# C attention's probabilities turned by VectorE and a scratch array instead of TensorE, in a two-layer streaming encoder

## The chip, the cores and the metric

One core of a Trainium2 chip. The metric is the device time of one execution in microseconds (us); lower is better. TensorE multiplies matrices, VectorE, ScalarE and GpSimd work on SBUF and PSUM, SyncE (its DMA queue is "SP") issues most transfers.

## The reference

Two layers over x of 1024 rows and 2048 columns, float32. Each layer projects x to 5376 columns, runs three branches, gates each, projects back to 2048 columns, adds 1.41 x and normalises.

```python
h = einsum('bsd,de->bse', x, w_in)      # a_v a_gate b_q b_k b_v b_gate c_q c_k c_v c_gate
a = pool_mixer(a_v, a_group_w, a_scale) * silu(a_gate)              # windows 2/4/8/16
b = swa_sink_attention(b_q, b_k, b_v, b_sinks) * silu(b_gate)       # 16 heads, 2 chunks, sinks
c = chunk_relbias_attention(c_q, c_k, c_v, c_rel_bias) * silu(c_gate)
x = layer_norm(alpha * x + einsum('bse,ed->bsd', concat(a, b, c), w_out), gain, bias)
```

The branch that matters here is C: 8 heads of 64; each chunk of 64 rows attends to itself and the 8 chunks before it, softmax over (q k / 8 + bias of the clipped distance), then times the values.

## The kernel before

Float32 numbers are split into a high and a low part; a product is three matmuls (high x high, high x low, low x high). Work is done in four steps `it`: a layer in two halves of 512 rows (`half(it)` is 0 or 1). Columns run along the partitions; a "unit" is a weight block of 128 x 512 which feeds 12 matmuls (four 128-row tiles of x, three each). The units pass a ring of four slots: SP loads `raw` (`load_unit`), ScalarE makes `wh` (`split`, L974), GpSimd `wl` (L1340), TensorE uses them (`project`).

A step's first part is four "pairs" `p`, each with 24 units for one group of A and two heads of C: `quarter(0..24)` are A's values, C's values, C's keys, C's queries, A's gate, C's gate, four units each (unit 24 is the next pair's unit 0). Then come 8 units for B's first query and keys (`KV0`), B (`B0`), and the output projection (`O0`). The pairs are a hardware loop on every engine but GpSimd, the order of the instructions in it is written by hand for each engine, and semaphores order the engines.

C's attention runs in four steps j of 128 queries for each of the pair's two heads: `c_scores` (TensorE, into `sc[h]`), `c_max` (VectorE: near bias, maximum), `c_exp` (ScalarE, into `prob`), `c_normalise` (VectorE), `c_transpose` (TensorE, 128x128 blocks of `prob` back into `sc[h]`, L681), `c_hi` (ScalarE, from `sc[h]`) and `c_lo` (VectorE, from `sc[h]` less the high part) into `pt`, `c_attend` (TensorE, `pt` times the values into `c_out[j]`), `c_low_rows` (ScalarE) and `c_add` (VectorE). A first half sees 1, 2, 3, 4 blocks of 128 keys in steps 0 to 3, a second half always 5. On TensorE step 0's scores follow unit 16, and step 3's attend follows unit 24, all within the pair; scores j+1 wait for `c_lo` of step j, since both use `sc[h]`. C's last attend, `c_out[3]`, uses a bank of `sc[0]`.

In steps 1 to 3 VectorE also does the layer norm of the step before, a quarter of the columns in each pair: `centre` (after the turn of C's values), `gain_and_bias` (its gain and bias are loaded into `prob`), and in steps 1 and 2 `turn_rows` (transposes in 32x32 blocks, stored in 128-byte pieces). A's mixer is a chain of VectorE operations after `av_ok`. Behind the pairs VectorE rotates B's first query and keys (`rotate`), makes their low parts (`keys_lo`, `rotated_query`) and turns B's values (L1699), before which TensorE does not start B's scores.

Of the kernel before, what the change touches and what calls it, by code (L numbers as in the profile page):

```python
# [29 lines left out]
F32 = mybir.dt.float32  # L30
F32R = mybir.dt.float32r
ALU = mybir.AluOpType
# [22 lines left out]
TWOS = B_TILES // 2  # L55
C_KEYS = 640
# [22 lines left out]
O0 = B0 + B_TILES * U_B  # L79
U_STEP = O0 + 4 * U_N  # L80

# [22 lines left out]
def build(nc, x, x_t, wall, a_gw, a_scale, sinks, rel_rev, ln_gain, ln_bias, rope_cos, rope_sin,  # L104
          pool_coef, pool_inv, out):
    with ExitStack() as ctx:
# [19 lines left out]
        bval_d = nc.dram_tensor("b_values_scratch", (DEPTH, CHUNK + SEQ, P), F32, kind="Internal").ap()  # L126
        tz_d = nc.dram_tensor("bias_rows_scratch", (DEPTH * 8, P * TZ), F32, kind="Internal").ap()
# [20 lines left out]
        bq0 = sb("bq0", [P, CHUNKS, 2, CHUNK], F32R)  # L148
        pt = sb("pt", [P, 5, 2, 2, P], F32R)
# [32 lines left out]


# [58 lines left out]
        c_out = [pv[:, 0:512], pv[:, 512:1024], pv[:, 0:512], sc[0][:, 0:512]]  # L242
# [62 lines left out]
        hist_in = sem("hist_in")  # L305
# [7 lines left out]
        ct_full = sem("ct_full")  # L313
# [60 lines left out]
        def last_rows(t, a, b):  # L374

            return sums[:, 4 * t:4 * t + 4, :].rearrange("p c n -> p (c n)")[:, a:b]

# [21 lines left out]
        def _(sp):  # L399
# [98 lines left out]
            for it in range(STEPS):  # L498
                with sp.Fori(0, C_PAIRS) as p:
                    for s in range(U_C):  # L500
                        if s == (4 if it else 0):

                            sp.wait_ge(gwl_ok, p + (C_PAIRS * it + 1))
                            sp.dma_start(gw[:], a_gw[layer(it), ds(p, 1)].rearrange("o c d -> (o c) d")
                                         ).then_inc(gw_in, 16)
                        if s == 9 and half(it):

                            sp.wait_ge(w_used, unit(it, p * U_C) + (2 + RING))
                            for m, a, b in ((mixh, 0, 3), (mixl, 3, 6)):
                                sp.dma_start(m[:, MIX_B:MIX_B + 2 * (b - a) - 1:2, :].bitcast(F32),  # L510
                                             hist_d[ds(p, 1), :, a:b, :].rearrange("o p a n -> (o p) a n")
                                             ).then_inc(hist_in, 16)
                        if s == 10:

                            sp.wait_ge(bias_ok, p + (C_PAIRS * it + 1))
                            if it:
                                sp.wait_ge(rope_ok, (B_TILES + 1) * it)
                                sp.wait_ge(bt_full, 2 * B_TILES * it)
                            else:
                                sp.wait_ge(tz_out, p * (16 * DEPTH) + 16 * DEPTH)  # L520
                            sp.dma_start(brope[:, 0, :].rearrange("p (h n) -> p h n", h=2),
                                         tz_d[ds(2 * p + 8 * layer(it), 2), 127:127 + P * (TZ - 1)]
                                         .rearrange("h (q c) -> q h c", c=TZ - 1)[:, :, 0:NEAR]).then_inc(bias_in, 16)
                        if s == 8 and it:

                            sp.wait_ge(w_used, unit(it, p * U_C) + (1 + RING))
# [1394 lines left out]
```

## Time and profile before

| | us |
|---|---|
| median of 3 runs | 2826.12 (2825.72 to 2827.51) |
| profiled execution | 2824.71 |
| its span | 2822.9 |
| TensorE busy | 2807.9 (99%) |
| VectorE busy | 1762.0 (62%) |
| ScalarE busy | 1297.4 (46%) |
| GpSimd busy | 1277.3 (45%) |
| DMA moved | 384.49 MB, 136 GB/s |

TensorE's granted clock was full in all 40 slices of the span. A row of a group gives what it wrote and read, the number of instructions, busy us and mean ns of one, then the idle time of the engine before them and who ended it. TensorE's matmuls are pipelined: one of 512 columns is listed with 0.39 us and the next starts 0.23 us later, so costs on TensorE are read from start to start.

### The profile page before, as it was taken

What the parts mean: (1) busy time and instruction counts of PE and PEld (TensorE: products, weight loads), DVE (VectorE), ACT (ScalarE), POOL (GpSimd) and SP (SyncE); (2) the same over time, 40 slices, a digit from 0 to 9 for tenths busy, and PEclk for the clock granted to TensorE, in tenths of its full rate; (3) what the DMA queues carried; (4) which work ended last, traced back from release to release, by engine and by line L of the source; (5) the groups of instructions that cost most, each with busy time, mean ns of one, the idle gap of its engine ahead of it and who ended that gap; (6) DMA issues with size and microseconds to landing.
All of it is one profiled execution on the core that took longest, in us unless ns stands there. A gap on an engine that the chain in (4) does not pass through costs nothing.

```text
span 2822.9 us, 45252 instructions
## 1 busy us (share of the span) xinstructions
PE 2807.9 (99%) x13316; PEld 2352.1 (83%) x13316; DVE 1762.0 (62%) x2950; ACT 1297.4 (46%) x2685; POOL 1277.3 (45%) x927
## 2 busy tenths in 40 slices
PE   9999999999999999999999999999999999999998
PEld 7888888888888888888888888888888888888886
DVE  5555679623777777862266666895137766678625
ACT  5444466523444445652244444664235444456521
POOL 4444444444444434444444444444444444444441
PEclk9999999999999999999999999999999999999999
DMA  6444332355555533335565663324564454333442
GB/s 212 132 133 131 100 89 82 112 175 176 169 168 167 162 91 98 86 94 179 172 192 172 174 173 105 86 82 133 155 214 133 129 155 151 100 86 84 136 157 101
DMA packets 311957, 384.49 MB, mean 136 GB/s; under 512 B 129408, under 2 KB 149920, under 8 KB 308128
## 3 DMA queue, kind: packets, MB, share of 16 engines
q1 hardware_dynamic: 308048, 367.26, 44.2%
q10 hardware_dynamic: 3792, 15.73, 1.4%
q8 instruction: 66, 1.08, 0.2%
q14 instruction: 51, 0.42, 0.0%
HBM read 327.23 MB, written 58.81 MB: 137 GB/s over the span
## 4 chain that ended last, share of the span: by engine, by line
PE 99%; DVE 0%; DMA 0%; issue 0%; ACT 0%; POOL 0%; SPq 0%; POOLq 0%
PE acc L639 70%; PE sc L639 18%; PE pv L639 9%; PE sc L681 2%; PE sc L718 1%; DMA raw<-in_wall 0%; DVE last_sums L1840 0%; DVE last_sums L1839 0%; POOL wl L1340 0%; DVE xl L1373 0%; SPq L489 0%; DVE av L1811 0%; DVE last_sums L1820 0%; ACT wh L974 0%; ACT xh L974 0%
## 5 line engine op out<-in xcount | busy, mean ns | idle before, releaser
L1340 POOL TENSOR_TENSOR wl<-raw,wh 128x512 fp32r<-128x512 f32 x920 | 1276.5, 1391 | 1501.9 <-ACT wh L974 1499.9
L974 ACT ACTIVATE wh<-raw 128x512 fp32r<-128x512 f32 x920 | 575.6, 630 | 1053.1 <-PE acc L639 722.3
L639 PE MATMUL acc<-xh,wh 128*128 128x512 f32 x2624 | 1034.0, 394 | 1.2 <-DVE xl L1373 1.2
L639 PE MATMUL acc<-xh,wl 128*128 128x512 f32 x2624 | 1022.7, 390 | 0.0
L639 PE MATMUL acc<-xl,wh 128*128 128x512 f32 x2624 | 1022.6, 390 | 0.0
L639 PEld LDWEIGHTS acc<-xh,wl 128*128 128x128 f32 x2624 | 492.6, 188 | 105.4
L639 PEld LDWEIGHTS acc<-xh,wh 128*128 128x128 f32 x2624 | 493.2, 188 | 98.2 <-DVE xl L1373 2.0
L639 PEld LDWEIGHTS acc<-xl,wh 128*128 128x128 f32 x2624 | 493.6, 188 | 94.0
L1373 DVE TENSOR_TENSOR xl<-prob,xh 128x512 f32 x48 | 55.6, 1158 | 235.8 <-ACT xh L974 235.8
L639 PE MATMUL sc<-wh,mixh 128*128 128x512 f32 x496 | 193.5, 390 | 0.1
L639 PE MATMUL sc<-wl,mixh 128*128 128x512 f32 x496 | 193.0, 389 | 0.0
L639 PE MATMUL sc<-wh,mixl 128*128 128x512 f32 x496 | 193.0, 389 | 0.0
L1373 DVE TENSOR_TENSOR pt<-sc,pt 128x512 fp32r<-128x512 f32 (+3 forms) x192 | 120.1, 663 | 80.7 <-ACT pt L974 79.7
L974 ACT ACTIVATE pt<-sc 128x512 fp32r<-128x512 f32 (+3 forms) x192 | 104.1, 577 | 82.2 <-PE sc L718 43.8
L1026 ACT ACTIVATE prob<-sc,nmax 128x640 f32<-128x640 f32 (+4 forms) x128 | 84.8, 662 | 71.9 <-DVE nmax L1426 70.0
L639 PEld LDWEIGHTS sc<-wh,mixh 128*128 128x128 f32 x496 | 93.1, 188 | 19.6 <-POOL wl L1340 0.5
L639 PEld LDWEIGHTS sc<-wh,mixl 128*128 128x128 f32 x496 | 93.1, 188 | 19.4
L639 PEld LDWEIGHTS sc<-wl,mixh 128*128 128x128 f32 x496 | 93.2, 188 | 19.1
L639 PE MATMUL acc<-wh,mixh 128*128 128x512 f32 x256 | 100.0, 391 | 0.0
L639 PE MATMUL acc<-wh,mixl 128*128 128x512 f32 x256 | 99.7, 389 | 0.0
L639 PE MATMUL acc<-wl,mixh 128*128 128x512 f32 x256 | 99.7, 389 | 0.0
L639 PE MATMUL pv<-wh,mixh 128*128 128x512 f32 x240 | 93.4, 389 | 0.0
(217 smaller groups left out, 3577.4 us busy)
## 6 DMA issues: line engine op xcount, KB each, us to landing
raw<-in_wall SPq DMA_DIRECT2D x920, 256.0 KB, 2.7
res_scratch<-res ACTq DMA_DIRECT2D x12, 1024.0 KB, 4.2
res<-res_scratch SPq DMA_DIRECT2D x12, 1024.0 KB, 4.9
res<-in_x SPq DMA_DIRECT2D x8, 1024.0 KB, 7.3
x_scratch<-res SPq DMA_DIRECT2D x8, 1024.0 KB, 5.2
x_t_scratch<-turned SPq DMA_DIRECT2D x128, 64.0 KB, 2.6
prob<-x_t_scratch SPq DMA_DIRECT2D x32, 256.0 KB, 2.8
res<-x_scratch SPq DMA_DIRECT2D x8, 1024.0 KB, 6.2
```

The source lines that it names most:

```text
L639: return nc.tensor.matmul(o, lhsT, rhs, start=start, stop=stop)
L681: last = nc.tensor.transpose(sc[h][:, cs], prob[:, h, cs], ident[:])
L718: last = nc.tensor.transpose(b_sc[g][:, u, c, :], probs(v, g)[:, u, c, :], ident[:])
L974: return nc.scalar.activation(o, i, ACT.Copy, scale=scale)
L1026: nc.scalar.activation(prob[:, h, c0:C_KEYS], sc[h][:, at:at + C_KEYS - c0], ACT.Exp, bias=nmax[:, h, 0:1], accum_out=psums[:, h, 0:1]).th ...
L1340: nc.gpsimd.tensor_tensor(wl[:, s, :], raw[:, s, :], wh[:, s, :].bitcast(F32), ALU.subtract).then_inc(w_lo, 1)
L1373: return V.tensor_tensor(o, whole, hi.bitcast(F32), ALU.subtract)
```

## The change

C's probabilities are no longer transposed on TensorE. VectorE turns `prob` in 32x32 blocks in place; SP stores it to a scratch array in DRAM with the blocks in their new places, one of four stores for each 32 partitions, and loads it again as `pt_raw` (the place of the low part in `pt`); `c_hi` and `c_lo` read `pt_raw`. The scores' banks are free after the exponents. A pair's four steps are spread: scores 0, 1, 2 follow units 16, 19 and 22, attend 0 follows unit 23; scores 3 follow unit 1 of the next pair, attends 1, 2, 3 its units 3, 6 and 10. The last pair's end lies among the first units of B. The loops over pairs are unrolled on all engines. The old keys and values of the second half are loaded by separate transfers; gain and bias are loaded at slot 13 of SP, behind the stores of step 3; gain and bias are applied as two operations with C's last sum between them.

```diff
+STORE_AT = (26, 29, 32, 36)
+LOAD_AT = (28, 31, 35, 38)
+        cprob_d = nc.dram_tensor("c_prob_scratch", (2, C_KEYS, P), F32, kind="Internal").ap()
+        pt_raw = nc.alloc_sbuf_tensor_at("pt_raw", [P, 5, 2, 2, P], F32, offset=pt_at)[:, :, :, 1, :]
-        c_out = [pv[:, 0:512], pv[:, 512:1024], pv[:, 0:512], sc[0][:, 0:512]]
+        c_out = [pv[:, 0:512], pv[:, 512:1024], pv[:, 0:512], pv[:, 512:1024]]
...
+            def store_c_prob(it, p, j, h):
+                n = c_step(it, p, j)
+                if n:
+                    sp.wait_ge(cp_in[h], 16 * n)
+                sp.wait_ge(cs_prob, 2 * n + h + 1)
+                c0 = 0 if half(it) else 512 - P * j
+                for r in range(4):
+                    rows = slice(32 * r, 32 * (r + 1))
+                    sp.dma_start(cprob_d[h, c0:C_KEYS, rows].rearrange("(m a) b -> a m b", a=32),
+                                 prob[rows, h, c0:C_KEYS].rearrange("a (m b) -> a m b", b=32)).then_inc(cp_out[h], 16)
+            def load_c_prob(it, p, j, h):
+                n = c_step(it, p, j)
+                sp.wait_ge(cp_out[h], 64 * (n + 1))
+                if n:
+                    sp.wait_ge(c_pv, n)
+                b0 = 0 if half(it) else 4 - j
+                sp.dma_start(pt_raw[:, b0:5, h, :], cprob_d[h, b0 * P:C_KEYS, :].rearrange("(c k) q -> k c q", k=P)
+                             ).then_inc(cp_in[h], 16)
+            def load_gain_bias(it, n):
+                if n:
+                    for h in range(2):
+                        sp.wait_ge(cp_out[h], 64 * c_step(it + 1, n, 0))
...
                 for h in range(2):
-                    pe.wait_ge(ct_lo, p * 8 + (8 * C_PAIRS * it + 2 * j + h + 1))
+                    if c_step(it, p, j):
+                        pe.wait_ge(cs_exp, 2 * c_step(it, p, j) + h - 1)
-            def c_transpose(it, p, j):
...
-                        last = nc.tensor.transpose(sc[h][:, cs], prob[:, h, cs], ident[:])
...
+                        quarter(1, 0)
+                        if p:
+                            c_scores(it, p - 1, 3)
+                        quarter(2, 0)
+                        quarter(3, 0)
+                        if p:
+                            c_attend(it, p - 1, 1)
...
+                    if p:
+                        c_attend(it, p - 1, 3)
+                    quarter(11, 0)
...
                     c_scores(it, p, 0)
+                    for s in range(17, 20):
+                        quarter(s, 0)
                     c_scores(it, p, 1)
...
+                    c_scores(it, p, 2)
                     quarter(23, 1)
+                    if half(it):
+                        pe.wait_ge(hist_values_in, p * 32 + (32 * C_PAIRS * layer(it) + 32))
+                    pe.wait_ge(v_ok, p + ((C_PAIRS + 1) * it + 1))
+                    c_attend(it, p, 0)
...
+                    if n:
+                        act.wait_ge(cp_out[h], 64 * n)
+                    act.wait_ge(cs_max, 2 * n + h + 1)
...
-                    copy(pth[:, b0:5, h, :], sc[h][:, b0 * P:5 * P].rearrange("p (b q) -> p b q", q=P)).then_inc(ct_hi, 1)
+                    act.wait_ge(cp_in[h], 16 * (c_step(it, p, j) + 1))
+                    copy(pth[:, b0:5, h, :], pt_raw[:, b0:5, h, :]).then_inc(ct_hi, 1)
...
+                    slot(22)
+                    slot(23)
+                    c_hi(it, p, 0)
+                    slot(24)
                     c_exp(it, p, 2)
                     mix_hi(p * 2 + (nb + 1), p + MIX_A)
+                    c_low_rows(it, p, 0)
...
-                    V.tensor_scalar(prob[:, h, c0:C_KEYS], prob[:, h, c0:C_KEYS], rinv[:, h, 0:1], None, ALU.mult
-                                    ).then_inc(cs_prob, 1)
+                    V_(V.tensor_scalar(prob[:, h, c0:C_KEYS], prob[:, h, c0:C_KEYS], rinv[:, h, 0:1], None, ALU.mult))
+                    V.transpose(prob[:, h, c0:C_KEYS], prob[:, h, c0:C_KEYS]).then_inc(cs_prob, 1)
...
+                    lo(ptl[:, b0:5, h, :], pt_raw[:, b0:5, h, :], pth[:, b0:5, h, :]).then_inc(ct_lo, 1)
```

VectorE's order in a pair is now: maximum 3 and c_lo 1 of the pair before, small copies, normalise 3, c_add 1, c_lo 2, the mixer's chain, c_add 2, the turn of C's values, centre, the mixer's low part, c_lo 3, the bias's preparation, gain, c_add 3 and C's product, bias, C's mix_lo, the keys' low part, turn_rows, values, queries, maximum 0, normalise 0, maximum 1, A's gate, normalise 1, c_lo 0, A's product, maximum 2, A's mix_lo, normalise 2, c_add 0, C's gate. Behind the last pair it is: maximum 3, c_lo 1, normalise 3, c_add 1, c_lo 2, rotate, c_add 2, the query's low part, rotate, c_lo 3, c_add 3, product, old keys, mix_lo, then keys_lo and the rest as before.

## Rows read from the trace of the kernel before

**Rows 1.** The page: the chain that ended last, shares of the span by line

```profile
PE acc L639 70%; PE sc L639 18%; PE pv L639 9%; PE sc L681 2%; PE sc L718 1%; DMA raw<-in_wall 0%; DVE last_sums L1840 0%; DVE last_sums L1839 0%; POOL wl L1340 0%; DVE xl L1373 0%; SPq L489 0%; DVE av L1811 0%; DVE last_sums L1820 0%; ACT wh L974 0%; ACT xh L974 0%
```

**Rows 2.** TensorE's groups by form: busy us, mean ns, idle before them

```profile
L681 PE MATMUL sc<-ident,prob 128*128 128x128 f32 x480 | 63.3, 273 | 0.0
```

**Rows 3.** Timeline of TensorE, pair 1 of step 1: start us, us, instructions

```profile
844.29 1.25 PE L681 MATMUL sc<-ident,prob 128*128 128x128 f32 x10
845.30 0.48 PE L639 MATMUL acc<-mixh,bq 128*128 128x512 f32 x1
845.61 0.40 PE L639 MATMUL acc<-mixl,bq 128*128 128x512 f32 x1
```

**Rows 4.** Three pairs of steps 0 and 1: us, then PE, PEld, DVE, ACT, POOL busy

```profile
84.70:304.80 220.10, 220.10 (x1043) 184.11 (x1042) 125.06 (x256) 99.38 (x201) 93.85 (x72) 1.00 0.45 130
778.25:1018.99 240.74, 240.74 (x1210) 204.72 (x1210) 176.75 (x301) 114.87 (x204) 106.03 (x72) 1.00 0.53 154
```

**Rows 5.** The chain in order of time: 16 units of TensorE

```profile
858.49 43.55 PE acc L639 x192
```

**Rows 6.** Timeline of VectorE, pair 2 of step 1

```profile
859.87 1.73 DVE L1406 TENSOR_TENSOR c_att<-c_low 64x128 f32<-64x128 f32 x2
...
868.00 1.56 DVE L1586 TENSOR_TENSOR s<-av 128x527 f32<-128x527 f32 x1 [3.65 <-ACT av L974]
...
874.70 0.28 DVE L1373 TENSOR_TENSOR bq<-gw,bq 128x128 fp32r<-128x128 f32 x1
...
878.23 3.01 DVE L1527 TENSOR_SCALAR res<-res,mv,rstd 128x512 f32<-128x512 f32 x4
881.57 1.38 DVE L1373 TENSOR_TENSOR mixl<-s,mixh 128x512 fp32r<-128x512 f32 x1 [0.32 <-ACT mixh L974]
...
893.74 2.49 DVE L1544 STREAM_TRANSPOSE turned<-res 128x512 f32<-128x512 f32 x4
...
902.71 0.11 DVE L1422 MEMSET sc<- 64x64 f32 x1 [1.32 <-PE sc L639]
...
905.54 0.15 DVE L1432 RECIPROCAL rinv<-psums 128x1 f32<-128x1 f32 x1
905.73 0.56 DVE L1433 TENSOR_SCALAR prob<-prob,rinv 128x640 f32<-128x640 f32 x1
...
933.91 0.68 DVE L1403 TENSOR_TENSOR c_low<-pv,c_low 64x512 f32<-64x512 f32 x1
934.63 0.59 DVE L1406 TENSOR_TENSOR c_att<-c_low 64x128 f32<-64x128 f32 x2
935.25 1.56 DVE L1373 TENSOR_TENSOR pt<-sc,pt 128x640 fp32r<-128x640 f32 x2
```

**Rows 7.** Timeline of GpSimd in the same pair

```profile
859.85 1.29 POOL L1340 TENSOR_TENSOR wl<-raw,wh 128x512 fp32r<-128x512 f32 x1 [1.53 <-ACT wh L974]
```

**Rows 8.** Timeline of ScalarE in the same pair

```profile
930.68 0.80 ACT L1026 ACTIVATE prob<-sc,nmax 128x640 f32<-128x640 f32 x1 [1.46 <-DVE nmax L1426]
...
935.44 0.63 ACT L974 ACTIVATE mixh<-tmp 128x512 f32 x1
```

**Rows 9.** Timeline of VectorE behind the pairs of step 1

```profile
1024.46 2.74 DVE L1671 CAST b_keys<-b_keys 128x64 fp32r<-128x64 f32 x4
...
1044.18 4.86 DVE L1373 TENSOR_TENSOR b_keys<-s,b_keys 64x512 fp32r<-64x512 f32 x4 [2.75 <-ACT b_keys L974]
1049.15 0.69 DVE L1514 SCALAR_TENSOR_TENSOR s<-acc,brope 128x512 f32<-128x512 f32 x1
...
1059.95 0.72 DVE L1699 STREAM_TRANSPOSE tmp<-sc 128x512 f32<-128x512 f32 x1 [3.46 <-PE sc L639]
```

**Rows 10.** SP's issues in that pair; engines meanwhile (last columns: DMA share, GB/s)

```profile
899.86 4.20 SPq L469 DMA_DIRECT2D x_t_scratch<-turned  x8
...
895.00:903.00 8.00, 8.00 (x40) 6.79 (x39) 3.53 (x9) 3.08 (x5) 3.72 (x4) 1.00 1.02 278
```

**Rows 11.** The page: DMA issues, KB each, median us from issue to landing

```profile
x_t_scratch<-turned SPq DMA_DIRECT2D x128, 64.0 KB, 2.6
```

More of the change, by code:

```diff
@@ L312, in build @@
         cs_prob = sem("cs_prob")
-        ct_full = sem("ct_full")
+        cp_out = [sem(f"cp_out{h}") for h in range(2)]
+        cp_in = [sem(f"cp_in{h}") for h in range(2)]
         ct_hi = sem("ct_hi")
@@ L1112, in pair @@
                     else:
-                        for s in range(2, 5):
-                            slot(s)
+                        slot(2)
+                        if p:
+                            c_hi(it, p - 1, 1)
+                        slot(3)
+                        if p:
+                            c_exp(it, p - 1, 3)
+                        slot(4)
                     used(it, p * U_C + (6 if first else 3))
@@ L1572, in _, with c_tail_product @@
                 pc, nb = C_PAIRS * it, 16 * it
-                per_c = 27 + (2 if it else 0) - half(it)
-                with dv.Fori(0, C_PAIRS) as p:
-                    section(p * per_c + total)
+                def c_tail_product(p, values):
+                    dv.wait_ge(c_fold, c_step(it, p, 3) + 1 + 2)
+                    attention_product(p * 2 + (MIXES * it + 2), values)
+                for p in range(C_PAIRS):
+                    section(total)
+                    if p:
+                        c_max(it, p - 1, 3)
+                        c_lo(it, p - 1, 1)
                     V.tensor_copy(coef1[:], coef[:, ds(p, 1), :].rearrange("p o n -> p (o n)"))
@@ L1583, in _ @@
                         V_(V.memset(av[:, 0:16], 0.0))
+                    if p:
+                        c_normalise(it, p - 1, 3)
+                        c_add(it, p - 1, 1)
+                        c_lo(it, p - 1, 2)
                     dv.wait_ge(av_ok, p + (pc + 1))
@@ L1624, in _ @@
                     if it:
-                        gain_and_bias()
-                        low_keys()
+                        gain()
+                    if p:
+                        c_add(it, p - 1, 3)
+                        c_tail_product(p - 1, p + (pc + 1))
+                    if it:
+                        bias()
+                    if p:
+                        mix_lo(p * 2 + nb, p - 1 + MIX_C)
+                    low_keys()
                     if turns(it):
@@ L1667, in _ @@
+                dv.wait_ge(rope_in, 32 * (it + 1))
+                rotate(it, 0, KV0 + 3, 0)
+                c_add(it, p, 2)
+                rotated_query(ROTS * it + 1, 0)
+                rotate(it, 1, KV0 + 7, 1, 1.0)
+                c_lo(it, p, 3)
+                c_add(it, p, 3)
+                c_tail_product(p, C_PAIRS * (it + 1))
                 dv.wait_ge(prod_ok, MIXES * it + 2 * C_PAIRS + 2)
```

318 lines of the change are left out of this document (160 added, 158 removed).

## Prediction, made before the changed kernel was run

> **What bounds the kernel now.** First the chain of work that ended last, by line: it is all TensorE's matmuls, 2% of it the transposes of L681 [rows 1]. Then the busy time of each engine over three C pairs: TensorE is busy in all of it (240.74 of 240.74 us), so it never waits inside the loops; a pair takes 73.4 us in the first half of the sequence (220.1 / 3) and 80.2 in the second half, and VectorE is busy 177 of 241 us in step 1 [rows 4]. (A step is one half of the sequence in one layer; steps 1 and 3 are second halves.) So time is won only where an instruction leaves TensorE, and lost where TensorE has to wait. Then TensorE's groups by form, for the 480 transposes of C [rows 2], and last the timelines of VectorE, ScalarE and GpSimd in one pair, since the question is who is late once TensorE is quicker.
>
> **What TensorE gets back.** Ten transposes of a second-half step of attention take 1.01 us from their start to the next matmul's, and that one lasts 0.31 us to the following start, where 0.23 is usual (a unit of 12 matmuls takes 43.55 / 16 = 2.72 us [rows 5]): 1.10 us. There are 32 such: 35.2 us [rows 3]. In a first half a pair has 20 transposes in four runs: by the same 0.10 each and 0.09 for a switch 2.4 us, in eight pairs 18.9. Together 54.1 us, which the chain's 2% bears out. The other matmuls stay in number and form; scores and attends stand apart now, at 0.01 to 0.09 us for a switch, and the transposes' own switches go: zero. Were all else hidden, the profiled execution would take 2824.7 - 54.1 = 2770.6 us (its span is 2822.9, and 1.8 lies around it); the median of the runs is 1.4 above it.
>
> **What is added.** VectorE gets 64 transposes of 128x640 in second halves and 64 smaller ones: four of 128x512 take 2.49 us now [rows 6], so 0.78 for 640, or by a whole single one 0.85; I take 0.85. The low part c_lo now comes from two SBUF tensors. From PSUM two of 640 took 1.56 us [rows 6]; two adds of c_att, with two SBUF inputs, took 0.59 us in one place and 1.73 in another [rows 6], and in the other GpSimd's split of a weight ran from 859.85 for 1.29 us [rows 7]. So such an operation of VectorE waits while GpSimd runs one: c_lo costs between nothing more and 1.3 us more for each split it meets. The Trainium skill has the rule ("SBUF — State Buffer", section "SBUF: two separate sides": the port pair that both share is an exclusive lock held for the whole instruction); the trace agrees, and the rule speaks against taking c_lo's input out of PSUM. ScalarE's high parts keep their size, but they wait for cp_in and the exponents for cp_out, and behind those on ScalarE stand the weights' splits: rival 3. SP issues 8 stores (0.52 us each, 4.20 for 8 [rows 10]) and 2 loads more for each step of attention, and waits for cs_prob with the units' loads behind it, some 5 us. A load is issued some four units ahead of its split and the splits run three units ahead of TensorE, so 5 us delay neither; without that cover each would be a us of TensorE. Gain and bias of the norm share prob, so their load moves behind the stores of step 3; centre, which needs them, comes some 15 us later: hidden, else it adds to the last attend. Unrolling: TensorE runs through the pair boundary without a gap now, so between 0 and 5 us for code that is fetched; I take 0.
>
> **Who is late: the attend of step 1.** Scores and attend take 1.2 us each in a second half: (80.25 - 24 x 2.72 - 4.4 - 0.7 for three more matmuls) / 8. Count from the end of unit 22. TensorE: scores 2, unit 23, attend 0, units 24 and 1, scores 3, units 2 and 3: attend 1 is wanted at 3 x 1.2 + 5 x 2.72 = 17.2, its second head at 17.8. VectorE and ScalarE: the split of unit 26 0.63 [rows 8], then GpSimd's 1.29, which c_lo(0) meets, so it starts at 1.95: +1.56 is 3.5; A's product 0.7, 4.2; maximum of step 2, 2.83 (902.71 to 905.54 [rows 6]), 7.0; its second exponent 0.8 and mix_hi 0.63 [rows 8], 8.5; mix_lo 0.7, 9.1; normalise 2 x (0.19 + 0.56 + 0.85) = 3.2, 12.3; c_add 1.34 (933.91 to 935.25), 13.7; gate 0.7, 14.4; maximum of step 3 2.83, 17.2; c_lo(1) 1.56, 18.8. That is 1.0 us late; with one split met on the way (+0.7, normalise under the split of slot 25) 1.7. It comes once in each of 8 second-half pairs: 13.6 us. In a first half the same chain with smaller blocks ends about 1 us before it is wanted: 0.
>
> **The attend of step 3.** From the end D of c_lo(1), VectorE: four small copies 0.35, normalise 3.2, c_add 1.34, c_lo(2) 1.56, the mixer's chain 6.7 (868.00 to 874.70), gw 0.3, c_add 1.34, turn of values 0.7, centre 3.0, ya_l 1.3, c_lo(3) 1.56: D + 21.3 [rows 6]. TensorE: second head of attend 1 0.6, units 4 to 7 10.9, attend 2 1.2, units 8 to 10 8.2: wanted at D + 20.9, the second head at D + 21.5. Undisturbed it just fits. But five groups in it (normalise, both c_add, both c_lo) can meet a split, which fills 1.3 of 2.7 us: some 0.4 us each, 2 us in all, so 1.8 us late. That holds for pairs 1 to 3 of the two second halves (only step 0 has no centre): 6 x 1.8 = 10.8 us. In step 2 the same sum with smaller blocks gives 0.7 us: 3 x 0.7 = 2.1. In step 0 nothing.
>
> **The tail of a step.** Pair 3's last attends now lie among B's first projections. After attend 3, VectorE has the wait for c_low 0.6, c_add 1.4, product 0.7, in a second half the key copies 2.74, the wait for ScalarE's keys 2.75, keys_lo 4.86, then rotation and sinks 7.34 (1049.15 until it was free, 3.46 before 1059.95), and the turn of B's values 0.7 [rows 9]: 21.1 us. TensorE needs that turn after B3, four value units and one quarter, 6 x 2.72 = 16.3: 4.8 us late; in a first half, mix_hi in place of the key copies, 19.0, 2.7 late. Now VectorE waits 3.46 us there, because keys_lo lies early. Two of each: 15.0 us.
>
> **Sum.** 2824.7 - 54.1 + 13.6 + 10.8 + 2.1 + 15.0 = 2812.1; with 1.4 for the median 2813.5. Forecast 2814; its own range, 0.6 us either way in each of 21 places, is 2801 to 2828.
>
> **Rivals.** (1) Both attends are in time and only the tail is late: 2826.1 - 54.1 + 15.0 = 2787 (2772 to 2801). For it: the chains are late by 1 to 2 us after a dozen terms, and splits may fall between VectorE's operations, as at 934 us [rows 6]. Against: 1.0 us of the first chain needs no split. (2) Slower: GpSimd's splits decide. If each chain meets one more whole split, (8 + 9 + 4) x 1.3 = 27 us, 2841 (2828 to 2856). For it: the mixer's first operation takes 1.56 us, the c_att adds 1.73 [rows 6], and much of what VectorE gets is of this kind. From 0.6 us more in each place on the change is slower than before. (3) The way through the scratch array is late. Normalised heads come out 7 and 9 us after the start of scores 0, eight issues bring SP to 11, landing takes 2.6 us for 64 KB [rows 11] and as much again for the load: 17 to 19 us, while ScalarE reads it at 20. The stores are 655 KB in 128-byte pieces; where such stores run now the engines' share is 1.02 at 278 GB/s [rows 10], so 2.4 us or more. If it is 3 us over in 8 second-half pairs, 24 us: 2838. The Trainium skill ("DMA: Bandwidth & Descriptors", section "Specifications") puts transfers under 512 bytes off line rate, as read-modify-writes; the rows show them only mixed with weights. (4) That the change saves TensorE nothing is out: the transposes are gone from its program.
>
> **Chances.** Forecast 0.43, rival 1 0.24, rival 2 0.19, rival 3 0.12, rest 0.02. A measurement of this kernel can tell 0.2%, 5.7 us, from no change: faster is under 2820.5, slower over 2831.8. Of the forecast's 0.43, 0.30 lies under and 0.13 between. Faster 0.30 + 0.24 = 0.54, same 0.13 and 0.02 of rivals 2 and 3, slower 0.31. Eight in ten need both sides: 2783 to 2848.
>
> **What would show it.** L681 gone, and C's transposes on VectorE at 0.85 us. Idle time of TensorE before matmuls out of pt, released by VectorE's L1373, 26 us in all: 1.7 in attend 1 of second-half pairs, near 2 in their attend 3, none in step 0. Idle time before B's first scores, released by VectorE's turn, 2.7 and 4.8 us. Periods of second-half pairs of 79.3 us in place of 80.2, VectorE busy some 69 us in them. Wrong if the periods are 75.9 (rival 1), if attends wait over 3 us behind a long c_lo (rival 2), or if ScalarE's reads of pt_raw wait for DMA (rival 3).

## The result, and the profile of the changed kernel

The changed kernel takes 2905.6 us (median of four runs, 2904.6 to 2910.3) against 2826.0 for the kernel before on the same chip: a ratio of 1.0284, 95% interval 1.0266 to 1.0302. It is 80 us slower, where 2814 was forecast and the range ended at 2848. The profiled execution has a span of 2908.2 us against 2822.9, and the rest goes by these two.

The page of the changed kernel: busy times, TensorE's slices, DMA packets, the chain by engine and by line (its first entries are those of [rows 1]), and the DMA issues (KB each, median us to landing).

```profile
PE 2789.8 (96%) x12836; PEld 2317.0 (80%) x12836; DVE 1883.3 (65%) x3078; ACT 1279.8 (44%) x2676; POOL 1283.6 (44%) x927
...
PE   8888999999988999999999999999999998999998
...
DMA packets 629706, 448.10 MB, mean 154 GB/s; under 512 B 385665, under 2 KB 467617, under 8 KB 625825
...
PE 75%; DVE 8%; DMA 8%; SPq 5%; issue 3%; ACT 1%; POOL 1%; ACTq 0%; POOLq 0%; DVEq 0%
...
c_prob_scratch<-prob SPq DMA_DIRECT2D x256, 80.0 KB, 2.3
pt_raw<-c_prob_scratch SPq DMA_DIRECT2D x64, 320.0 KB, 4.9
```

TensorE's group of transposes [rows 2] is gone and it still idles 2908.2 - 2789.8 = 118 us, where it idled 15 (all but 3 us of that behind its last matmul). The chain was TensorE alone in [rows 1]; a quarter of it is something else now, DMA and SP's queue 13%. There are 385665 packets under 512 B; the kernel before had 129408.

The changed kernel's waits: engine, line, for whom; us in total, times, longest.

```profile
ACT pt L1029 <- DMA pt_raw<-c_prob_scratch: 87.8, 40, 6.5
PE pv L697 <- DVE pt L1450: 80.5, 33, 7.8
...
ACT wh L1029 <- DMA raw<-in_wall: 76.8, 22, 12.0
...
ACT prob L1084 <- DMA c_prob_scratch<-prob: 61.1, 42, 3.8
```

TensorE stands before its attends for VectorE's low part, which stands for ScalarE's high part, which stands for the load out of the scratch array. That is the third rival's sign. Two stretches show how. First step 0, pair 1, in the timelines of SP, ScalarE (with its queue) and TensorE, in one window (PE, PEld, DVE, ACT, POOL busy, then clock, DMA share, GB/s), and in the DMA view of 107 to 111 us (median us to landing of what is issued there):

```profile
97.91 9.20 SPq L475 DMA_DIRECT2D c_prob_scratch<-prob  x8
107.15 2.79 SPq L428 DMA_DIRECT2D raw<-in_wall  x2
110.03 7.99 SPq L485 DMA_DIRECT2D pt_raw<-c_prob_scratch  x2
118.07 0.97 SPq L428 DMA_DIRECT2D raw<-in_wall  x2
...
97.84 3.78 ACTq L1160 DMA_DIRECT2D bias_rows_scratch<-bias_row_scratch  x2
...
118.85 0.63 ACT L1029 ACTIVATE wh<-raw 128x512 fp32r<-128x512 f32 x1 [11.47 <-DMA raw<-in_wall]
...
122.18 1.19 PE L697 MATMUL pv<-pt,mixh 128*128 128x256 f32 x4 [7.37 <-DVE pt L1450]
...
109.00:127.00 18.00, 10.63 (x45) 8.74 (x44) 5.92 (x12) 4.04 (x7) 3.99 (x4) 0.81 0.58 161
...
raw<-in_wall SPq DMA_DIRECT2D x2, 256.0 KB, 11.0
pt_raw<-c_prob_scratch SPq DMA_DIRECT2D x1, 256.0 KB, 10.6
c_prob_scratch<-prob SPq DMA_DIRECT2D x1, 64.0 KB, 12.7
```

The eight stores take SP 9.2 us where 4.2 had been measured [rows 10], and one of them is 12.7 us on its way; the second head's load has to wait for it. The weights issued next, at 107.15, land at 118.8, and ScalarE waits 11.5 us for them; the first head's load, issued behind them at 110.03, lands at 120.7, and TensorE's attend, which waits 7.4 us, hangs on that. In this stretch the granted clock is 0.81: behind the wait matmuls start 0.43 us apart for a few us (the 1.2 GHz level) where 0.23 is usual. Such stretches cost some 13 us in the whole run (each start's excess over 0.227 us, added up). The DMA view of the same stretch, 97 to 119 us, in 40 slices:

```profile
DMA  9967987541161116211621166998731111111112
GB/s 326 210 179 220 178 157 152 104 93 48 46 144 54 48 48 137 61 46 48 142 56 45 48 78 150 406 342 267 239 100 48 46 48 48 46 48 50 48 51 96
...
raw<-in_wall SPq DMA_DIRECT2D x4, 256.0 KB, 7.2
...
pt_raw<-c_prob_scratch SPq DMA_DIRECT2D x2, 256.0 KB, 7.2
```

The engines are not full there. In about half of the slices they are busy to 0.1 at some 48 GB/s, one or two of sixteen, while everything is awaited. (The two medians of 7.2 us are the middle of landings of 10 to 12 us and of some 4 us for what is issued when the broadcast ends.)

Second, step 1, pair 2, timelines of SP, ScalarE, VectorE and TensorE, then the DMA view of 886 to 909 us:

```profile
899.39 2.42 SPq L485 DMA_DIRECT2D pt_raw<-c_prob_scratch  x2
901.86 2.17 SPq L428 DMA_DIRECT2D raw<-in_wall  x1
908.01 4.40 SPq L475 DMA_DIRECT2D c_prob_scratch<-prob  x8
...
915.69 0.43 SPq L499 DMA_DIRECT2D prob<-in_ln_bias  x1
...
908.02 0.74 ACT L1029 ACTIVATE pt<-pt_raw 128x640 fp32r<-128x640 f32 x1 [6.52 <-DMA pt_raw<-c_prob_scratch]
...
908.79 1.77 DVE L1450 TENSOR_TENSOR pt<-pt_raw,pt 128x640 fp32r<-128x640 f32 x2 [5.76 <-ACT pt L1029]
...
921.80 1.92 DVE L1604 TENSOR_SCALAR res<-res,mv,rstd 128x512 f32<-128x512 f32 x4 [2.84 <-DMA prob<-in_ln_bias]
...
909.76 0.87 PE L697 MATMUL pv<-pt,mixh 128*128 128x256 f32 x5 [3.55 <-DVE pt L1450]
```

```profile
q1 hardware_dynamic: 9634, 5.66, 87.9%
...
pt_raw<-c_prob_scratch SPq DMA_DIRECT2D x2, 320.0 KB, 8.8
```

Here the queue is full (88% of 16 engines' time) with stores in 128-byte pieces, 1 MB of the norm's rows, 1 MB of history keys and the bias rows, and the load lands after 8.8 us.

### The profile page after: what moved, and what is told of

The parts are those of the page before. It is cut to its first block, busy times and chain, and to the rows that moved or that the text cites. A ratio compares the mean times of both kernels' runs of the same rounds, so it can differ in the third digit from the quotient of the medians.

```text
span 2908.2 us, 41599 instructions
## 1 busy us (share of the span) xinstructions
PE 2789.8 (96%) x12836; PEld 2317.0 (80%) x12836; DVE 1883.3 (65%) x3078; ACT 1279.8 (44%) x2676; POOL 1283.6 (44%) x927
## 2 busy tenths in 40 slices
DMA packets 629706, 448.10 MB, mean 154 GB/s; under 512 B 385665, under 2 KB 467617, under 8 KB 625825
## 4 chain that ended last, share of the span: by engine, by line
PE 75%; DVE 8%; DMA 8%; SPq 5%; issue 3%; ACT 1%; POOL 1%; ACTq 0%; POOLq 0%; DVEq 0%
PE acc L697 50%; PE sc L697 15%; PE pv L697 9%; DMA pt_raw<-c_prob_scratch 3%; SPq L475 3%; DMA prob<-in_ln_bias 1%; DVE mixl L1450 1%; DMA raw<-in_wall 1%; DMA c_prob_scratch<-prob 1%; PE sc L766 1%; SPq L428 1%; SPq L513 1%; DVE pt L1450 1%; POOL wl L1417 1%; DVE prob L1512 0%
## 5 line engine op out<-in xcount | busy, mean ns | idle before, releaser
L1450 DVE TENSOR_TENSOR pt<-pt_raw,pt 128x640 fp32r<-128x640 f32 (+4 forms) x128 | 98.2, 798 | 91.8 <-ACT pt L1029 90.5
L697 PE MATMUL pv<-pt,mixh 128*128 128x256 f32 x240 | 45.2, 312 | 77.8 <-DVE pt L1450 77.8
L1029 ACT ACTIVATE pt<-pt_raw 128x640 fp32r<-128x640 f32 (+4 forms) x128 | 72.7, 596 | 98.2 <-DMA pt_raw<-c_prob_scratch 87.8
L697 PEld LDWEIGHTS pv<-pt,mixh 128*128 128x128 f32 x240 | 36.8, 206 | 93.6 <-issue 92.0
L697 PEld LDWEIGHTS sc<-wh,mixh 128*128 128x128 f32 x496 | 93.1, 188 | 19.6 <-POOL wl L1417 0.5
```

The source lines that it names most:

```text
L697: return nc.tensor.matmul(o, lhsT, rhs, start=start, stop=stop)
L1029: return nc.scalar.activation(o, i, ACT.Copy, scale=scale)
L1450: return V.tensor_tensor(o, whole, hi.bitcast(F32), ALU.subtract)
```

## The experiments

The last four columns say what each step costs against the kernel before, from the start of the last unit of each step in the two profiled executions (us); the first is the median's distance from the kernel before on the same chip, and the four add up to it within some 6 us.

| kernel | against before | step 0 | 1 | 2 | 3 |
|---|---|---|---|---|---|
| changed kernel | +79.7 | +30.5 | +20.8 | +15.9 | +18.6 |
| no way through the array | +6.2 | +17.5 | -1.8 | -3.5 | -3.3 |
| one large store a head | +22.3 | +24.6 | -1.8 | -2.7 | +2.3 |
| four large stores a head | +45.8 | +23.6 | +7.4 | +12.4 | +2.9 |
| stores without loads | +24.8 | +27.1 | -4.1 | +4.8 | -2.8 |
| bias rows early | +62.1 | +12.6 | +19.0 | +13.9 | +18.7 |
| bias rows early, two arrays | +48.3 | +13.1 | +13.6 | +10.2 | +12.7 |
| broadcast spread | +47.7 | -2.0 | +15.8 | +19.6 | +16.4 |
| spread, two arrays | +36.3 | -3.7 | +14.7 | +11.7 | +9.4 |
| no way, spread | -14.4 | -3.9 | -1.6 | -3.5 | -3.2 |

**Is it the way through the array?** Theory: rival 3, the transfers. Rival: VectorE is late (rivals 1 and 2). First the changed kernel without them:

```diff
-    sp.dma_start(cprob_d[...], prob[...]) x4; sp.dma_start(pt_raw[...], cprob_d[...])
-    copy(pth[:, b0:5, h, :], pt_raw[:, b0:5, h, :])
+    copy(pth[:, b0:5, h, :], pt[:, b0:5, h, 1, :].bitcast(F32))    # same size, constant
```

> The changed kernel without the way through DRAM: no store of the turned probabilities and no load of pt_raw, c_hi and c_lo read the low part's place in pt instead (so C's probabilities are wrong numbers), the exponents wait for the normalising of the step before. VectorE's transposes and its c_lo from SBUF stay. Theory 1 (what cost the 80 us is the way through the scratch array and SP's queue): the waits of attends 2 and 3 for it go, VectorE's own lateness as I summed it stays, 2805 to 2835 us. Theory 2 (VectorE's added work and its collisions with GpSimd): the time stays above 2885 us. Between 2835 and 2885 both have a share.

2832.3 us, ratio 1.0019 (1.0009 to 1.0028). That is in the range of theory 1. So 73 of the 80 us are the transfers, and steps 1 to 3 come out below the kernel before. Step 0 stays at +17.5.

**Which part of the way?** Large pieces in the same region and of the same size, first as one store a head, then as four:

```diff
-                for r in range(4):
-                    rows = slice(32 * r, 32 * (r + 1))
-                    sp.dma_start(cprob_d[h, c0:C_KEYS, rows].rearrange("(m a) b -> a m b", a=32), ...
+                sp.dma_start(cprob_d[h, c0:C_KEYS, :]....rearrange("(p n) -> p n", p=P), prob[:, h, c0:C_KEYS])
```

> The changed kernel with one store for each head, of the same bytes to the same region, in rows of 512 to 2560 bytes for each partition in place of four stores in 128-byte pieces (so the probabilities come back in wrong places). Loads and all waits stay. If the small pieces and SP's eight issues make the way late: about half of the loss comes back, 2850 to 2870 us. If it is the latency of two transfers and the order of SP's queue, whatever the pieces: above 2890 us.

> The changed kernel with its four stores per head kept in number, bytes and place, but each moving 32 whole rows of prob into one contiguous piece of the scratch array, so no piece is 128 bytes; what is loaded back is therefore not the turned block. Theory A, the pieces: the time is that of the run with one large store per head, 2848 us (2843 to 2856), SP's four more issues a head costing nothing that TensorE sees. Theory B, the issues: SP takes about 0.5 us for each, its loads of weights stand behind, and most of the 57 us between the changed kernel and the large single store stays: 2885 to 2905. Between the two, each us over 2848 goes to the issues.

2848.4 and 2872.1 us (1.0076, 1.0059 to 1.0092; 1.0168, 1.0151 to 1.0185). The first is 2 us below the range for small pieces and issues together; the second lies between its two theories, which share the price. A ladder: transfers in one large store 16 us, four issues in place of one 24, pieces of 128 bytes in place of large ones 34. Then the stores alone:

```diff
-                    sp.wait_ge(cp_in[h], 16 * n)
+                    sp.wait_ge(cp_out[h], 64 * n)
...
-                sp.dma_start(pt_raw[:, b0:5, h, :], cprob_d[h, b0 * P:C_KEYS, :]...
...
-    copy(pth[:, b0:5, h, :], pt_raw[:, b0:5, h, :])
+    copy(pth[:, b0:5, h, :], pt[:, b0:5, h, 1, :].bitcast(F32))
```

> The changed kernel without the 64 loads out of the scratch array: c_hi and c_lo read a constant block in place of what came back, all stores of 128-byte pieces stay, and the exponents still wait for their landing. The run with neither is 2832 us, the changed kernel 2905. Theory A, the way through the array is late (store, landing, load, landing, one after the other): most of the 73 us goes with the loads, 2840 to 2860, and what stays is the exponents' wait for prob. Theory B, the stores harm by what they do to the others (SP's queue, weights' loads behind them, the engines' read-modify-writes): 2880 to 2900, TensorE's waits then moving to units whose weights are late.

2850.9 us (1.0091, 1.0075 to 1.0108), theory A. In steps 1 to 3 stores alone cost nearly nothing (-4.1, +4.8, -2.8 against -1.8, -3.5, -3.3): what costs there are the loads, 57 of the 61 us that they add to the span lying in those three steps. By the waits above that is because they come back late; this run alone does not part that from what stands behind them in SP's queue. In step 0 the stores alone cost 10.

Then the gain and bias load that was moved behind the stores, left out, so that the norm multiplies by and adds what lies in prob:

```diff
                     if s == 13 and it:
-                        load_gain_bias(it - 1, p)
+                        pass
```

> The changed kernel without the two broadcast loads of the norm's gain and bias, so centre waits for its input rows alone and gain and bias multiply by what lies in prob. Waits of TensorE before attend 3 in steps 1 to 3 are 23.7 us in all in the changed kernel and 5.1 us without the way through the scratch array. Theory A, centre is late because this load stands behind the landing of the fourth step's stores: the waits fall to some 8 us, 2890 (2884 to 2895). Theory B, attend 3 is late because its own blocks come late out of the scratch array: 2902 to 2906, no change. Step 0 keeps its time under both.

2899.3 us (1.0264, 1.0247 to 1.0281): 6 us, at neither theory's number, and no more than the two intervals leave open. centre has no wait left (VectorE stood 19 us for it in all), but TensorE's waits before attends are 77.7 us in all where they were 80.5, and many are still 2.6 to 3.6 us. In pair 2 of step 1 the load for attend 3 now lies there in time (landed at 919.3, wanted by VectorE at 922.2); what stays is attend 2's wait for its load, and VectorE's chain that starts late behind it. The moved load was not hidden from VectorE, but it was not the cause.

**Step 0.** There ScalarE's queue issues the broadcast of the next pair's bias rows. Issue it behind slot 17 of the pair before:

```diff
-                        if it == 0:
-                            bias_rows()
...
                     slot(17)
+                    if it == 0 and p + 1 < C_PAIRS:
+                        act.wait_ge(bias_in, 16 * (p + 1))
+                        bias_rows(p + 1)
```

> The changed kernel, where in step 0 ScalarE's queue issues the broadcast of a pair's bias rows some 12 units earlier, away from the stores of the fourth attention step; nothing else is altered. In the changed kernel step 0 costs 30.5 us more than in the kernel before, 7.5 us of it in each of pairs 1 to 3 at the attend of step 3, with landing of the stores taking up to 12.7 us while the broadcast runs. Theory A, the broadcast holds up the stores: those waits fall under 2 us each, 17 to 22 us less: 2884 to 2889. Theory B, the 128-byte pieces and SP's issues do it alone: 2900 to 2910, waits of 7 us as before. The other steps keep their times under both.

2888.4 us (1.0223, 1.0196 to 1.0250), theory A: step 0 falls from +30.5 to +12.6, the others stay. The four runs of this kernel lie from 2881.3 to 2898.4, so the total is loose; the steps are those of an execution at the median. SP's eight stores take 4.21 us again:

```profile
102.21 4.21 SPq L475 DMA_DIRECT2D c_prob_scratch<-prob  x8
```

The other suspect in step 0 was a move that the prediction overlooked: the keys' low part (low_keys) now stands behind VectorE's wait for the bias rows in step 0 too. In the kernel without the way, VectorE and TensorE in pair 0:

```profile
54.55 0.62 DVE L1700 TENSOR_SCALAR brope<-brope 128x256 f32<-128x256 f32 x2 [13.32 <-DMA brope<-bias_rows_scratch]
...
58.14 0.80 PE L681 MATMUL acc<-xh,wh 128*128 128x512 f32 x1 [4.12 <-DVE mixl L1436]
```

Undone in the changed kernel, without the way, and with the early broadcast:

```diff
+                    if it == 0:
+                        low_keys()
                     dv.wait_ge(bias_in, p * 16 + (16 * pc + 16))
...
-                    low_keys()
+                    if it:
+                        low_keys()
```

> The changed kernel with one move undone: in step 0 VectorE makes the keys' low part before it waits for the bias rows, as in the kernel before. The wait of TensorE before unit 16 in pair 0 of step 0 (4.1 us) should go: 2901 (2898 to 2904) if the later pairs, in which the wait for attend 3 covers it, keep their times; 2895 if the shorter way of VectorE helps them too. Rival: the keys are not late for this move but because VectorE itself is late; then 2905 and the wait stays at 4.

> The run without the way through the scratch array (2832 us), with one more move undone: in step 0 VectorE makes the keys' low part before it waits for the bias rows. Left out are the stores and loads of the scratch array, so the second products are not of the turned block. In that run TensorE waits 4.12, 2.04, 2.69 and 2.73 us before unit 16 of the four pairs of step 0, released by VectorE's low part of the mixed keys. Theory A, these are the price of that move: 11.6 us of waits and some 6 us of matmuls at half clock behind them go, 2815 to 2821, which is the blind forecast's 2814 without its transfers. Theory B, VectorE is late in step 0 anyway and the wait moves to another place (attend 1 or 3, or the bias rows' maximum): 2828 to 2833. With the changed kernel itself the same move gained 0 to 6 us, since there the waits for the fourth step lay behind it.

> The whole changed kernel with both moves: bias rows broadcast some 12 units earlier in step 0, and the keys' low part made ahead of the wait for them. With the first alone 2888 us. Theory A, what is left of step 0 is then the wait of 4.25 us before unit 16 and its matmuls at half clock: 2881 to 2885. If the two add to nothing, 2888. Neither can reach the 2826 of the kernel before, since the steps 1 to 3 keep their 55 us.

2905.1, 2818.2 and 2892.1 us. Without the way it gives 14 us (0.9970, 0.9960 to 0.9980) as theory A had it. In the changed kernel it gives nothing. That is the rival's time, though not for the rival's reason, for TensorE's wait of 4 us in pair 0 does go. With the early broadcast it gives nothing either (2881 to 2888 had been expected): other waits of step 0 take its place. But both step 0 findings hang on one thing, that the bias rows land late, and the DMA view above says why. The broadcast is issued with the two heads as the outer dimension. One pattern turned round, nothing moved:

```diff
-    act.dma_start(tz_d[heads].rearrange("h (q c) -> h q c", c=TZ),
-                  rel_d[heads].rearrange("h (o c) -> h o c", o=1).to_broadcast([2, P, TZ])
+    act.dma_start(tz_d[heads].rearrange("h (q c) -> q h c", c=TZ),
+                  rel_d[heads].rearrange("h (o c) -> o h c", o=1).to_broadcast([P, 2, TZ])
```

> The changed kernel with one address pattern altered: the broadcast of a pair's bias rows (two issues by ScalarE's queue, same bytes, same place in the order) runs over the 128 copies first and the two heads second, in place of the heads first. In the changed kernel the engines' share is 0.1 at 46 to 48 GB/s for most of 12 us while it runs, about two of the sixteen, and loads issued meanwhile land after 7.2 us in place of 2.8. Theory A, two engines do the broadcast and all other transfers wait for their part on those two: spread over sixteen it takes 1 to 3 us, the three waits of 7.4 to 7.8 us in step 0 go, 2883 to 2890, as with the broadcast issued earlier, and SP's eight stores issue in some 4 us in place of 9.2. Theory B, what crowds is the 128-byte pieces and the amount of data: 2900 or more.

2873.8 us (1.0161, 1.0143 to 1.0179), 32 us less, more than theory A asked. ScalarE's queue is through with the two issues in 1.22 us where it took 3.78, the broadcast's packets run for 5 us (95.9 to 101.2) where they ran for 20 (99.3 to 119.1), and the DMA view of the same stretch (96 to 118 us) shows it:

```profile
94.58 1.22 ACTq L1160 DMA_DIRECT2D bias_rows_scratch<-bias_row_scratch  x2
```

```profile
DMA  6998799996476799599999999993069899884000
...
raw<-in_wall SPq DMA_DIRECT2D x7, 256.0 KB, 3.6
pt_raw<-c_prob_scratch SPq DMA_DIRECT2D x2, 256.0 KB, 4.0
```

In the pairs of step 0 TensorE has no wait of 0.3 us or more left once the first 11 us are over, with the stores in 128-byte pieces and the moved low_keys in place: pairs 1 to 3 gain 2.2 to 2.3 us each on the kernel before, where the prediction gave 2.4 for 20 transposes. One detail went otherwise: SP's eight stores still took 7.6 us there, so the narrowness of the broadcast alone is not what makes them slow to issue. The Trainium skill ("DMA: Bandwidth & Descriptors", section "Why a DMA increments its semaphore by 16 and not by 1") says that a transfer is spread over the largest number of engines up to 16 that divides the outermost dimension of both sides: two heads, two engines. The trace agrees, at 46 to 48 GB/s and a share of 0.1. The kernel before has the same narrow broadcast, 20 us long, but could not gain by this turn: its TensorE waits 3 us in all, in the first 10 us of the run.

**Steps 1 to 3.** Two scratch arrays in turn, so that a store need not wait for the last load's landing (upon the early broadcast):

```diff
-                if n:
-                    sp.wait_ge(cp_in[h], 16 * n)
+                if n > 1:
+                    sp.wait_ge(cp_in[h], 16 * (n - 1))
-    cprob_d[h, ...]
+    cprob_d[2 * (n % 2) + h, ...]
```

> The whole changed kernel with the bias rows broadcast earlier (2888 us), and the scratch array doubled: steps of attention take turns, so a store waits for the load of the step before the last and not for the last one, which was issued one unit ahead of it and takes 4.9 to 8.6 us. Theory A, SP's waits for that landing (42 us in the changed kernel, 28 of them) delay the next stores and with them the next load: without them loads land 2 to 4 us earlier, TensorE's waits before attends 2 and 3 in steps 1 to 3 (some 30 us) fall by half, 2868 to 2878. Theory B, the length of the way itself decides (eight issues, landing, load, landing), and SP only waits there in place of later: 2883 to 2893.

2874.9 us (1.0170, 1.0153 to 1.0187), theory A in the total: 13.5 us less, nearly all of it in steps 1 to 3. SP's waits of that kind, in the changed kernel and here:

```profile
SPq L475 <- DMA pt_raw<-c_prob_scratch: 42.1, 28, 4.7
```

```profile
SPq L475 <- DMA pt_raw<-c_prob_scratch: 7.5, 20, 1.2
```

Then, upon that, the loads of the history keys and of the bias rows two units later, behind the third load:

```diff
-                    if s == 10 and half(it):
+                    if s == 12 and half(it):
...
-                    if s == 10:
+                    if s == 12:
```

> The run with two scratch arrays and the early broadcast (2875 us), with the loads of the history keys (two of 512 KB) and of the bias rows (256 KB) issued two units later in every pair, behind the load of the third attention step and not ahead of it. Theory A, in steps 1 and 3 the third load is late because it stands behind these: it lands in 4 to 6 us in place of 8.8, and TensorE's waits before attend 2 (0.6 to 2.2 us in 6 places) go: 2866 to 2872. Rival, the keys or the bias rows are then late themselves, or attend 3 waits longer by as much: 2873 to 2880.

2905.8 us (1.0284, 1.0266 to 1.0302), 31 us worse, worse than the rival said. The bias rows are then late themselves; VectorE stands for them 13 us in step 0, and keys and attends stand behind it in every step:

```profile
132.61 0.62 DVE L1714 TENSOR_SCALAR brope<-brope 128x256 f32<-128x256 f32 x2 [13.16 <-DMA brope<-bias_rows_scratch]
```

The order that was tried only changed who waits. The sums of these steps:

> The whole changed kernel with the broadcast spread (at its own place), two scratch arrays and the history keys and bias rows two units later. If each mends what it is for: 2860 to 2870. The lower end is set by the run without any transfer of the scratch array, 2832; the kernel before is at 2826, which this cannot reach.

> As the one before it, and in step 0 the keys' low part ahead of the wait for the bias rows. Without any transfer that move gained 14 us, with the early broadcast it lost 4 (within its spread). With a broadcast that no longer holds up the loads it should gain some of it: 2850 to 2860; if exponents still wait for the stores' landing in step 0, as they did with the early broadcast, nothing: 2860 to 2870.

> The whole changed kernel with the broadcast of the bias rows spread over the copies (2874 us alone) and two scratch arrays in turn (13 us less where the broadcast was merely early). Theory A, they act in different steps and add: 2859 to 2865, step 0 without a wait of TensorE in its pairs. Theory B, the spread broadcast leaves nothing for the second array to mend: 2870 to 2875. Under both it stays slower than the 2826 of the kernel before.

2893.0, 2881.0 and 2862.3 us. The first missed its range by 23 us and the second by 11 to 21; both carry the later keys, and the third, which differs from the first in that alone, is 31 us faster. Between the first two the undone low_keys gives 12 us, since the bias rows are late again there. The third, 1.0141 (1.0119 to 1.0163), has its median at theory A, but its runs lie from 2856.6 to 2872.6, so that how much the second array adds to the spread broadcast is loose. It is the best whole form of the change that was found, still 36 us behind the kernel before. None beats it.

**The blind sum without transfers.** Last, neither stores nor loads, and the broadcast spread:

> The changed kernel with neither stores nor loads of the scratch array (their second products are not of the turned block) and the broadcast spread. The keys' low part stays behind the wait for the bias rows, as in the change. Theory A, that move costs only because the narrow broadcast lands late: its waits of 2.0 to 4.1 us before unit 16 go without undoing it, step 0 ends at -5 to -7 us against the kernel before, and the whole is 2808 to 2814, the blind forecast's 2814 or a little under. Theory B, the move costs by itself: 2825 to 2832.

2811.7 us (0.9949, 0.9932 to 0.9965), theory A; step 0 ends at -3.9 where -5 to -7 had been expected. TensorE in step 0's tail, before attends 1 and 3 in step 1 and in that step's tail, and a window of one pair:

```profile
342.65 0.73 PE L681 MATMUL sc<-b_keys,bq 128*128 128x128 f32 x4 [1.89 <-DVE tmp L1786]
...
854.37 0.83 PE L681 MATMUL pv<-pt,mixh 128*128 128x256 f32 x5 [1.63 <-DVE pt L1436]
...
876.80 0.82 PE L681 MATMUL pv<-pt,mixh 128*128 128x256 f32 x5 [0.62 <-DVE pt L1436]
...
1053.93 1.22 PE L681 MATMUL sc<-b_keys,bq 128*128 128x256 f32 x4 [2.97 <-DVE tmp L1786]
...
771.10:849.60 78.50, 76.25 (x364) 64.05 (x364) 67.03 (x109) 36.61 (x67) 34.40 (x24) 1.00 0.56 159
```

**Two halves of the change by themselves.** In the kernel before, TensorE's transposes left out (the high and low parts are taken from the scores where they lie), and, in another kernel, VectorE's transposes added behind normalise with everything else kept (what TensorE then turns is already turned in blocks):

```diff
-    c_transpose: up to five transposes by ident a head
+    c_transpose: its waits and its signal alone
```

```diff
-    V.tensor_scalar(prob[...], prob[...], rinv[:, h, 0:1], None, ALU.mult).then_inc(cs_prob, 1)
+    V_(V.tensor_scalar(prob[...], prob[...], rinv[:, h, 0:1], None, ALU.mult))
+    V.transpose(prob[...], prob[...]).then_inc(cs_prob, 1)
```

> The kernel before without TensorE's 480 transposes of C: c_hi and c_lo read the scores in place (wrong numbers; the mask value is -1e4 so that they stay finite). It prices the first term of my sum alone: 2826 - 54 = 2772 us if no other engine is late behind it. If VectorE or ScalarE limit as soon as TensorE is quicker, 2790 us or more.

> The kernel before with VectorE's transposes in 32x32 blocks added behind each normalising (TensorE's transposes stay; the result is in wrong places). Theory 1: VectorE's 0.85 us a head are partly on the way to TensorE's transposes in this tight order; at most 64 x 1.6 = 51 us if all of it is on the way, and I expect 2830 to 2855 us. Theory 2 (VectorE's work alone makes the change slow): 2880 us or more.

2798.7 us (0.9899, 0.9883 to 0.9916) and 2867.4 us (1.0144, 1.0127 to 1.0161). The first is in the range for other engines being late: in the old order half of the 54 us is lost at once. TensorE waits 20 us between its matmuls where it waited 3, most of it where one pair goes over into the next, for VectorE's normalise (13.6 us in 24 places), as in

```profile
845.11 0.49 PE L639 MATMUL acc<-xh,wh 128*128 128x512 f32 x1 [0.92 <-DVE prob L1428]
```

Some 10 us of the loss no wait shows. VectorE's turns cost 41 us there, between the two theories (2855 and 2880): TensorE's transposes wait for them, 1.7 us in one place of a second-half pair and 0.7 in another. If the two halves added up, the old order would take 2826 - 27 + 41 = 2840 us (an estimate; it was not run), where the new order without transfers takes 2811.7. So the spreading over 18 units earns its place.

## Why the prediction was wrong, point by point

The kernel without transfers and with the broadcast spread is the one to hold against the sum, since the sum had no term for either; without transfers alone the time is 2832.3.

**What TensorE gets back: right.** Without transfers a second-half pair has TensorE busy 76.25 us where it was 80.25 [rows 4]; 4.0 of the predicted 4.4, and the rest is two attends whose two halves take 0.14 us longer when they come straight after a wait. First-half pairs gain 2.2 against 2.4.

**Attend of step 1: right.** 1.63 us for 1.7, in eight places. **Attend of step 3: right in kind, a third in size.** 0.62 us for 1.8 in six places, and 0.48 in step 2 for 0.7 in three: the splits, charged at 2 us a chain, seem to cost less, though no run takes them by themselves. **Tail: right in place, two thirds in size.** 2.97 and 1.9 us for 4.8 and 2.7. These were put 7 + 1 + 5 us too dear. Against that stands what no term had: 4.7 us of matmuls at half clock, nearly all behind the tails' waits, 2 us of attends after a wait, 0.8 at the start, and some 6 that I can't place. So the sum, 2812.1 for the profiled execution, is what that kernel gives (2810.3 and 1.8 around it), and that it agrees so closely is luck: by step, -6.8, -0.6, -4.6, -0.6 were predicted and -3.9, -1.6, -3.5, -3.2 measured.

**VectorE's price: right.** 0.85 us for a transpose of 640, and 67.0 us busy a pair for 69.

```profile
887.78 0.85 DVE L1512 STREAM_TRANSPOSE prob<-prob 128x640 f32<-128x640 f32 x1
```

**The way through the array: the failed step.** The sum put this way at nothing. The mechanism stood there as rival 3, at a chance of 0.12 and 24 us. The transfers cost 73 us as the kernel stands (2905.6 - 2832.3) and 62 with the broadcast spread (2873.8 - 2811.7); transfers and narrow broadcast together are 94 (2905.6 - 2811.7), 21 of them there without any transfer, through the moved low_keys. These things were wrong.

It took 2.6 us for each landing, the median of 64 KB stores [rows 11], and judged 17 to 19 us against 20. For the stores that was about right: their median is 2.3, and the eight in the full window of [rows 10] had landed after 2.0. It was the loads that were mis-sized, with a row of 64 KB for loads of 320 KB: their median is 4.9, and those that decide land after 7 to 9 (10.6 in step 0). The rows to read were those of the loads beside which they are issued; in the kernel before:

```profile
mixl<-hist_scratch SPq DMA_DIRECT2D x8, 768.0 KB, 9.0
...
brope<-bias_rows_scratch SPq DMA_DIRECT2D x16, 256.0 KB, 5.4
```

It looked at second halves alone and gave step 0 nothing. Step 0 has a broadcast that no row of the prediction showed, because in the kernel before it hindered nobody: weights issued while it runs land there after 5 to 10 us, and TensorE, for which they are issued units ahead, does not wait. The changed kernel is the first to need a load within a few us of its issue while that broadcast holds two engines. Spreading it gives 32 us with the transfers and 21 without.

**SP's issues and waits, and the load of gain and bias, both called hidden: wrong for SP, open for the load.** SP's in-order waits are worth 11 to 14 us (two arrays), and three more issues a head 24 with large pieces; the gain and bias load is worth 6, which is not clear of the spread. **The moved low_keys was overlooked:** 14 us without transfers, nothing once the broadcast is spread.

**What was said would show it:** ScalarE's reads of pt_raw waiting for DMA was named as the sign of rival 3, and is the largest wait of any compute engine for a transfer. The 0 us taken for unrolling the loops stays open: no run has the change with its loops kept.

The Trainium skill's rule on transfers under 512 bytes ("DMA: Bandwidth & Descriptors", section "Specifications"), which the prediction cited and did not price, goes the same way as the 34 us between four stores of large and of 128-byte pieces; in step 0 with the spread broadcast the same pieces cost TensorE nothing.

## What to carry to other kernels

A way out of and back into the core costs two landings in the state that the queue will be in, so take landing times from transfers of the same size and of the stretch that the new one meets, not from the median of smaller ones, and ask of every transfer already there what it occupies, how many engines and for how long, even if nobody waits for it now. When an added transfer comes into a schedule with little slack, look first at broadcasts with a small outer dimension; turning one pattern round gave more here than any reordering. And price a moved wait in every stage in which it stands, also in the one that the diff changes by a single line.

## What the runs showed of the hardware

A DRAM-to-DRAM broadcast of 2 x 384 KB with two heads outermost kept about two of sixteen engines busy at 46 to 48 GB/s for 20 us, and loads issued on another queue in the middle of it landed after 10 to 12 us (median of the stretch 7.2, of the run 2.8); with 128 copies outermost it took 5 us, and the stretch's loads landed after 3.6. SP needed 0.53 us an issue for eight 128-byte-piece stores without the broadcast beside them (4.21 us), 1.15 (9.20 us) beside the narrow and 0.95 (7.59 us) beside the spread one; what makes those issues long was not taken apart. TensorE's granted clock was 0.81 over 18 us with a wait of 7.4 us in them, its matmuls starting 0.43 us apart before they came back to 0.23.
